# Identity matmuls on TensorE ahead of three waits for normalised rows: a two-block transformer on one core

## What is computed

```
def first_block(...):
    for l in range(DEPTH):
        mix = hybrid_mixer(x, tabs, w_in[l], ...)          # first step: x @ w_in[l]
        x = layer_norm(DEEPNORM_ALPHA * x + mix, ln1_g[l], ln1_b[l])
        moe = hier_moe(x, ...)
        x = layer_norm(DEEPNORM_ALPHA * x + moe, ln2_g[l], ln2_b[l])

def sq_relu_mlp(h, w1, w2):
    return jnp.square(jax.nn.relu(h @ w1)) @ w2

def second_block(...):                                     # i = 0: GLA, i = 1: SSD
        hl = layer_norm_2(DEEPNORM_ALPHA_2 * hl + m_l[2] * snake(yl), ...)
        hl = layer_norm_2(DEEPNORM_ALPHA_2 * hl + m_l[5] * sq_relu_mlp(modulate(hl, m_l[3], m_l[4]), ...), ...)
```

## Time and profile before

| what | value |
|---|---|
| median of 3 runs | 2380.19 us (2379.17 to 2384.97) |
| the profiled execution's own time | 2382.67 us |
| its span, first to last instruction | 2381.1 us |
| TensorE busy | 2093.6 us, 88% of the span |
| VectorE busy | 1172.8 us, 49% |
| ScalarE busy | 661.5 us, 28% |
| mean granted TensorE clock | 0.951 of full speed |

### The profile page before, as it was taken

One profiled execution on the slowest core, in us unless ns is written; L12 is line 12 of the kernel. 1 busy time (PEld: TensorE's weight loads), 2 busy tenths in 40 slices (PEclk: granted clock), 3 DMA queues, 4 the chain that ended last, 5 costly groups with the idle time before them and its releaser, 6 DMA issues.

```text
span 2381.1 us, 31809 instructions
## 1 busy us (share of the span) xinstructions
PE 2093.6 (88%) x11894; PEld 1435.9 (60%) x11894; DVE 1172.8 (49%) x2135; ACT 661.5 (28%) x1234; POOL 164.1 (7%) x151
## 2 busy tenths in 40 slices
PE   5998888888998847886999879999979997998997
PEld 2477432324586412323788758888867785765896
DVE  1046411112063401215738577666676886845766
ACT  1054210011252200112433321111124545732332
POOL 1000200001001100002341300000000000000000
PEclk9999999999998979998899889999989998999999
DMA  5349699983469678984221223213222234314552
GB/s 187 136 173 335 234 404 412 397 335 123 145 224 309 243 280 339 413 332 143 77 83 71 71 88 124 106 71 106 79 75 94 75 122 156 128 71 142 194 190 111
DMA packets 154016, 440.38 MB, mean 185 GB/s; under 512 B 12384, under 2 KB 14864, under 8 KB 145536
## 3 DMA queue, kind: packets, MB, share of 16 engines
q1 hardware_dynamic: 145792, 416.98, 47.2%
q0 software_dynamic: 8064, 21.28, 2.9%
HBM read 534.52 MB, written 1.21 MB: 225 GB/s over the span
## 4 chain that ended last, share of the span: by engine, by line
PE 39%; DVE 7%; ACT 3%; DVEq 3%; issue 1%; DMA 1%; ACTq 0%; SPq 0%; POOL 0%; POOLq 0%
PE bank L2024 23%; PE bank L2115 11%; PE bank L2166 5%; DVE ARENA L3130 1%; ACT ARENA L2668 1%; PE bank L2029 1%; DVE UT L2752 1%; DVEq L2754 0%; DVE XLO L2755 0%; DVEq L2742 0%; DVE UL L2755 0%; DVE XA L2743 0%; DMA W<-in_ffn_w 0%; ACT ARENA L2424 0%; ACT ARENA L2661 0%
## 5 line engine op out<-in xcount | busy, mean ns | idle before, releaser
L479 PE MATMUL bank<-WD,XT 128*128 128x512 f32 (+1 forms) x576 | 244.1, 586 | 6.6 <-ACT XT L807 4.8
L628 PE MATMUL bank<-WA,XG 128*32 128x512 f32 x1536 | 184.0, 623 | 74.5 <-DMA WA<-in_expert_w_up 62.9
L2457 ACT ACTIVATE WPH<-W 128x1024 fp32r<-128x1024 f32 x128 | 135.5, 1063 | 406.4 <-PE bank L2024 207.1
L479 PEld LDWEIGHTS bank<-WD,XT 128*128 128x128 f32 x576 | 110.9, 193 | 137.4 <-issue 130.0
L2024 PE MATMUL bank<-UH,WPH 128*128 128x512 f32 (+1 forms) x512 | 174.1, 340 | 6.7 <-DVE UL L2755 3.1
L2024 PE MATMUL bank<-UL,WPH 128*128 128x512 f32 (+1 forms) x512 | 172.8, 338 | 0.0
L2024 PE MATMUL bank<-UH,WPL 128*128 128x512 f32 (+1 forms) x512 | 172.7, 337 | 0.0
L628 PEld LDWEIGHTS bank<-WA,XG 128*32 128x32 f32 x1536 | 47.2, 114 | 200.2 <-issue 120.9
L2793 DVE TENSOR_TENSOR WPL<-W,WPH 128x1024 fp32r<-128x1024 f32 x128 | 153.4, 1219 | 17.7 <-ACT WPH L2457 17.7
L2115 PE MATMUL bank<-WPH,MHH 128*128 128x512 f32 x384 | 149.5, 389 | 0.0
L2115 PE MATMUL bank<-WPL,MHH 128*128 128x512 f32 x384 | 149.5, 389 | 0.0
(11 more groups left out here) (428 smaller groups left out, 3760.4 us busy)
## 6 DMA issues: line engine op xcount, KB each, us to landing
WA<-in_expert_w_gate SPq DMA_DIRECT2D x32, 2048.0 KB
WA<-in_expert_w_up SPq DMA_DIRECT2D x32, 2048.0 KB
WC<-in_expert_w_down SPq DMA_DIRECT2D x32, 2048.0 KB
W<-in_ffn_w SPq DMA_DIRECT2D x64, 1024.0 KB, 6.7
WD<-in_ada_w SPq DMA_DIRECT2D x48, 1024.0 KB, 7.0
WA<-in_expert_w_gate SPq DMA_DIRECT2D x64, 512.0 KB
WA<-in_expert_w_up SPq DMA_DIRECT2D x64, 512.0 KB
WC<-in_expert_w_down SPq DMA_DIRECT2D x32, 1024.0 KB
```

The lines of the kernel that those rows point to most:

```text
L479: last = nc.tensor.matmul(bank[r.bank(key)][:, 0:n], lhs[k], rhs[k], start=(k == 0), stop=(k == len(lhs) - 1))
L628: last = nc.tensor.matmul(bank[r.bank(key)][32 * g:32 * g + 32, :], xg[:, 4 * part + k, col:col + 32], WA[part][:, g, :, k, :], start=(par ...
L2457: nc.scalar.activation(piece_view(WPH, q), piece_src(i, q), ACT.Copy).then_inc(hi_done, 1)
```

## The change

At each of the three places TensorE now multiplies `ident` by `ident` (128 columns) into the bank that the turns are about to fill, ahead of the wait: 10 times in each of the two layers of the first network, 20 times ahead of "f0", and 10 times ahead of "m1". For this the claim of the bank moves ahead of the wait as well. Nothing is removed, and the last feed-forward part ("f1") and the first turns of the second network ("m0") stay as they are.

```
+            def keep_busy_short(key, n):
+
+                for _ in range(n):
+                    nc.tensor.matmul(bank[r.bank(key)][:, 0:P], ident[:], ident[:], start=True, stop=True)
...
                         if n == 0:
+                            if t == 0:
+                                r.claim(pe, ("xT", 0, 0), l)
+                                pe.nop(nofuse=True)
+                                keep_busy_short(("xT", 0, 0), 10)
                             pe.wait_ge(x_ready, 2 * TT * l + t + 1)
...
+        IDLE_TURNS = {"f0": 20, "m1": 10}
...
+            def keep_busy(key, n):
+
+                for _ in range(n):
+                    nc.tensor.matmul(bank[r.bank(key)][:, 0:P], ident[:], ident[:], start=True, stop=True)
+
             def turned_x(tag, nt, snaked, before):
 
                 for s in range(nt // 2):
+                    if s == 0 and tag in IDLE_TURNS:
+                        r.claim(pe, ("uT", tag, 0, 0))
+                        keep_busy(("uT", tag, 0, 0), IDLE_TURNS[tag])
                     if before is not None:
                         pe.wait_ge(x_rdy, before + 2 * s + 2)
```

## The result

The changed kernel takes 2388.15 us (median of 14 runs, 2380.85 to 2396.6). The kernel before, run beside it, takes 2381.28 (14 runs, 2377.51 to 2385.16). The ratio is 1.0031, with a 95% interval of 1.0018 to 1.0044: 4.3 to 10.5 us slower, about 6.9. The forecast was 2381.4 with a range up to 2386.0, so the median lies outside it, and on the slow side. The prediction had called 0.3% what a measurement of this kernel can tell from no change; the result sits on that line.

The account below looks back on a forecast made before the run. The prediction took the kernel as bound mostly by TensorE's chain of work, with the clock dipping only in single slices. Its terms, 0 - 2.7 + 4.65 - 0.7 = +1.25 us on the median 2380.19, gave 2381.4, range 2377.5 to 2386.0.

Parts of the forecast that it names:

- The identity's price: One 128x128 identity, two records, was reckoned at 0.233 us at full clock: 2.3 us for ten, 4.65 for twenty.
- The forecast of waits at "f0": At "f0" ScalarE and VectorE would wait 9.0 us instead of 4.4; TensorE's 14.8 us idle between the halves would stay.
- Layer 0, 0: First network, layer 0: ten identities hidden by the input's DMA, first product slow as before; no change, 0 us.
- "f0", +4.65: Ahead of the first half's turns at "f0", with no idle time there, twenty identities delay everything behind by 4.65 us.
- "m1", -0.7: At "m1" ten identities bring the clock up earlier for the first half: 0.7 us gained, bounds -2.0 and +2.7.
- The good bound of 2.0: Best case at "m1": clock still full, first half in 3.9 us instead of 6.46, 2.0 us gained.
- Layer 1, -2.7: Head of layer 1: ten identities hidden in TensorE's idle time keep the clock up for the first product, 2.7 us gained.
- a rival for a failed gain here: Layer 1: the break behind the turns still lowers the clock before the product; sum +4.0, 2384.1 us, chance 0.2.
- The rule on turns: Layer 1: turns do not count as TensorE being busy as matmuls do, so the break would run 540.3 to 544.48.
- the forecast's base: The median of the runs shown of the kernel before, 2380.19 us, to which the sum of +1.25 was added.
- the bounds of the four places: Limits per place: layer 0, 0 to 2.9 gained; layer 1, 0 to 2.7 gained; "f0", 0 to 4.65 lost; "m1", -2.0 to +2.7.

Follow-up runs that it names:

- the change with 13: The changed kernel with 13 identities instead of 10 ahead of "m1": 2389.29 us, ratio 1.0034 against the kernel before; measured again, 2388.32 us, 1.0033.
- the control: The changed kernel's code with an empty table and no identities, so TensorE's instructions are those of the kernel before: 2383.69 us, ratio 1.0002.

## Why the prediction was wrong

**The identity's price: right.** 0.233 us at full clock was reckoned. Twenty took 4.63, which is 0.232 each (0.223 from one start to the next). The forecast of waits at "f0" (9.0 us for ScalarE and VectorE) came out as 8.56 and 8.52, and the 14.8 us between the halves stayed. The Trainium skill's figure for a matmul of 128 columns with its weight load ("TensorE: Matmul & The Clock Gate", "Back-to-back issue gap") would have made it 3.2, an estimate; the trace does not agree with it, and its 4.63 us decides.

**Layer 0, 0: right.** The identities took 4.61 us at half clock in the shade of the input's DMA, and the product was slow as before.

**"f0", +4.65: right.** 4.5 in all seven profiles that have it.

**"m1", -0.7: right as to its place.** Without "f0" it gained 0.65 in all three profiles, and as reckoned: with only "m1" the clock fell as before, at 1754.4, and was back at 1757.9 where before it was back at 1761.4. Within the change it gained 2.2, 2.2 and 0.9 by the product behind the turns: the stretch at half clock that starts at 1754.5 before is missing in the first two, so the identities run at full clock. The good bound of 2.0 was drawn 0.2 too tight for that. A part of it is not the identities' work: the delay from "f0" alone gives -0.7 by 1790 us.

**Layer 1, -2.7: this step failed.** The prediction said that the ten run "from about 538.0 to 540.3, inside the idle time that ends at 542.04" and named VectorE's norm as their cover. Measured is +0.8 to +1.4 in the eight profiles with identities at the head of the round, 1.1 on average: 3.8 us off. The trace of before named the norm as the releaser of those 4.05 us. It was not what held TensorE. The norm ended at 541.49 and the turns started 0.55 us later, while at "f0" the second half's turns start at 1396.40, 0.06 us after their norm, and two other turns behind the same line as here (L1025) start 0.14 us after it (270.12 and 790.78):

```profile
1395.53 0.81 DVE L2735 TENSOR_SCALAR XA<-XA,MV,ST 128x1024 f32<-128x1024 f32 x1
```

So the rows held the warning, and the prediction did not ask what the half microsecond was. In the eight profiles with no identities at this place the norm ends 3.50 us behind the last sum and the turns start 3.97 to 4.46 behind it; in the eight with identities at the round's head these start 3.84 to 4.46 behind the sum, released by "issue":

```profile
539.66 3.31 PE L570 MATMUL bank<-ident 128*128 128x128 f32 x20 [3.84 <-issue]
```

(the first profile of the change with 13). The same identities in front of the loop's branch start 0.35 us behind the sum, so what is shown is that the step to the next round holds TensorE. Why is not shown: that instructions are fetched in that time is likely (the trace has two 16 KB transfers of an instruction queue in this stretch, before and after) but is argued. I had a rival for a failed gain here, +4.0 in all, but with another cause, the clock; and the product did run at full clock.

The rule on turns that stood with that rival (the Trainium skill, "TensorE: Matmul & The Clock Gate", "Part 4: PE-mode transpose") is not settled. In the change there was no break ahead of the turns. With identities at the round's end there was one: from 540.61 to 544.65 TensorE ran turns and nothing else, and the clock fell at 545.1, as by that rule; but it also stood idle for 1.93 and 1.04 us of that time, so the two cannot be told apart.

**What the sum left out.** The three places measured give +1.1, +4.5 and -2.1 (mean of three profiles), or +3.5. That would have been 2383.7 beside the forecast's base, inside the range. The rest is in work that the change doesn't touch, and it has two parts.

One is shown. A shift of a few tenths decides at the stop behind 1800 whether the clock falls, at a price of 4.6 us for it and the fall behind it near 1840 (2.6 to 2.7 and 1.6 to 1.7). Ten identities at "m1" alone put the kernel 0.33 us early against those moments and turn a gain of 0.65 into a loss of some 4; twelve do not. In the changed kernel the fall came in two profiles of three: 3.5 us on average from 1768 to 1900.

The other is an association. From 560 to 1379 us the eight profiles with identities at the layers' heads have -1.1 us on average against the profile of before (deviation 3.5), the ten without have -3.9 (deviation 3.2): 2.8 us more, with an uncertainty of some 1.6. Two stretches in it stand apart. From 880 to 960 us the eight lose 2.9 to 3.9 us each, with the clock at half for 13.7 us near 890 and once more near 930; of the ten, nine lie between -0.9 and +0.1 and the control has +2.2. From 960 to 1080 four of the eight lose 3.5 to 7.0 us, and these four have the falls between 1006 and 1066; the other four and the ten have 0.5 at most. Against that, the eight gain 3.6 us more than the ten from 560 to 760, where single profiles differ by 9. That looks like the same mechanism at other stops, but no kernel here moved those stops alone, so it stays a reading.

With both, and +0.9 behind 1900, the sum is 3.5 + 3.5 + 2.8 + 0.9 = +10.7, where the two measurements of the change are +6.9 and +7.8. It mixes what it compares with: the 2.8 is against ten profiles, the rest against the one of before, and the ten have +0.8 behind 1900 as well. Straight against the profile of before, the three spans of the change are +10.9, +9.5 and 0.0 us, 6.8 on average, and that profile is 1.4 above its own median. With three profiles of a thing that scatters by 4 us, such sums are good to some 3 us. They say where the loss sits, not its last microsecond.

**What stays open.** In what share of its executions the changed kernel has the falls: three profiles are too few to say. That 13 identities at "m1" don't help its median is less of a riddle. From 1740 to 1900 us the change costs 2.7, 2.6 and -1.0 us, 1.4 on average, and with 13 it is -0.6, -0.6 and 2.8, or 0.5: the gain to be expected is 0.9 us, less than a median can tell. The executions of that kernel range from 2380.68 to 2400.32 us, wider than before's 2375.94 to 2389.1 beside them. And no version here beats the kernel before beyond the measurement: the best are those with identities at the round's end (0.999, 0.9974 to 1.0006) and with 12 at "m1" (1.0003).

The range was wrong with the sum: it was made from the bounds of the four places only. A term for "the clock falls at other stops than before" was missing, 3.5 us on average behind 1768 and perhaps some 3 more in the expert part, and two stops in the trace of before would have warned: the stops of 3.2 us behind 1800 and of 2.2 us in the expert part, of the same kind as the idle times of 4.05 and 2.32 us in or right behind which the clock did fall.

## What to carry to other kernels

Work put into an idle time must be free to start when it begins. Look for every condition that ends it, not only the one that the profile names: the bank (11.4 of 14.8 us gone between the halves of "f0"), and the step from one round of a hardware loop to the next (3.8 to 4.5 us for TensorE here). A releaser that had ended half a microsecond before its waiter started, where such a pair takes 0.06 to 0.15 elsewhere, is not the one.

Filling a stop to keep the clock up buys at most what that stop loses, 2.7 us at the first product of layer 1, and moves everything behind it. Where later stops are on the edge of a fall, a gain of 0.65 us can cost 4; so judge such an edit by many executions, and compare by stretches, since two profiles of the same instructions (before and the control) differed by 3.4 us between 560 and 1379 us.

## What the runs showed of the hardware

- From one round of the layer loop to the next TensorE starts nothing for 3.84 to 4.46 us (eight profiles with identities at the head); with 3.36 us of identities in front of the branch there are still 1.93 and 1.78 us behind them.
- The granted clock fell or not in one and the same stop of 3.22 us, with the same work ahead, by a difference in alignment of 0.2 to 0.6 us against before. Each of the eighteen profiles stood on the side of the line, between 1802.34 and 1802.51, that its alignment says.
- A delay of 3.1 us at 1783 us, without any other change, brought the same two falls as ten identities at "m1".
- What a fall costs: 2.6 to 2.7 us at the stop behind 1800, where the clock was at half for 6.8 us, and 1.6 to 1.7 near 1840, where it was for 3.4.
- A 128x128 identity in float32, two records, takes 0.223 us from one start to the next at full clock (twenty at "f0").
